# A hybrid decoder layer on one core: input projection in other passes, its norm moved behind the matmuls, the front of tile 1 and the output stages moved along the expert slots

## The reference

```python
xn = rms_norm(x, attn_norm)
proj = xn @ w_in                       # 3328 columns: q 512, k 512, v 512, p 1792
q = rope(q, pos); k = rope(k, pos)
o_da = attend(q, k, v, lam)            # differential attention, 4 heads; samples read a paged cache
o_rw, wkv, shift = rwkv_time_mix(p, shift0, wkv0, ...)   # 8 heads of 64, state carried along time
h = x + concatenate([o_da, o_rw]) @ w_out
h = h + peer_ffn(rms_norm(h, ffn_norm), peer_wq, sub_keys, peer_u, peer_v)
y = rms_norm(h, final_norm)
```

## Time and profile before

| | |
|---|---|
| median of 3 runs | 4260.41 us (4252.23 to 4271.85) |
| the profiled execution, its own time | 4256.56 us |
| its span in the profile | 4254.8 us |
| first matmul of the projection | 32.37 us |
| first expert gather (POOL) | 848.52 us |
| busy over the span | PE 68%, DVE 61%, POOL 31%, ACT 27% |
| expert gathers | 1088, 1157.7 MB of 1445.2 MB moved |
| TensorE clock granted, mean | 0.769 of full speed |

### The profile page before, as it was taken

The page is one execution under the profiler, slowest core; times in us unless marked ns, Lnnn a source line. Parts: engine busy times, 40 slices in busy tenths (PEclk is TensorE's granted clock), DMA queues, the critical chain, the costliest instruction groups (busy, mean ns, idle before and its releaser), DMA issues.

```text
span 4254.8 us, 53587 instructions
## 1 busy us (share of the span) xinstructions
...
## 2 busy tenths in 40 slices
...
DMA  7355714599999999999999999999999667999998
GB/s 259 129 174 190 264 36 167 197 401 384 418 380 408 401 412 367 413 416 379 404 413 414 378 404 406 403 379 413 403 364 387 207 233 270 355 364 419 419 410 347
DMA packets 319382, 1445.20 MB, mean 340 GB/s; under 512 B 28228, under 2 KB 64196, under 8 KB 179478
## 3 DMA queue, kind: packets, MB, share of 16 engines
...
## 4 chain that ended last, share of the span: by engine, by line
DMA 34%; PE 30%; DVE 23%; issue 5%; ACT 4%; POOL 3%; SPq 0%; DVEq 0%; ACTq 0%; POOLq 0%
DMA pe_buf<-in_experts,pe_idx 20%; DMA op_wkr<-scratch_wk_rows 10%; DVE pe_buf L2187 10%; PE ip_B L961 9%; PE pe_B L1292 4%; PE pe_psO L1342 4%; PE pe_B L1275 3%; POOL pe_buf L914 2%; PE pe_psH L1324 1%; PE pe_B L1246 1%; PE pe_B L997 1%; DMA tm_ps<-in_x 1%; ACT pe_Z L1644 1%; POOL at_vp L874 1%; DMA op_w<-in_w_out 1%
## 5 line engine op out<-in xcount | busy, mean ns | idle before, releaser
L914 POOL DMA_INDIRECT pe_buf<-in_experts,pe_idx x1088 | 1260.4, 1158 | 2750.4 <-PE pe_psO L1342 1717.0
L2187 DVE CUSTOM_DVE_ANT_0 pe_buf<-pe_buf,pe_hnR 128x1024 f32<-128x1024 f32 x1088 | 1315.1, 1223 | 886.3 <-DMA pe_buf<-in_experts,pe_idx 723.0
L1342 PE MATMUL pe_psO<-pe_buf,pe_Z 128*32 128x256 f32 x8704 | 791.6, 496 | 758.3 <-ACT pe_Z L1644 738.1
L1342 PEld LDWEIGHTS pe_psO<-pe_buf,pe_Z 128*32 128x32 f32 x8704 | 270.6, 131 | 1286.2 <-ACT pe_Z L1644 1014.6
L1636 ACT ACTIVATE pe_gelu<-pe_dot 128x2 f32<-128x2 f32 x544 | 110.2, 203 | 1678.1 <-DVE pe_dot L2187 1677.7
L961 PE MATMUL ip_B<-ip_w,ip_xT 128*128 128x512 f32 (+1 forms) x1008 | 421.7, 571 | 5.8 <-DMA ip_w<-in_w_in 4.0
L1324 PE MATMUL pe_psH<-pe_hn,pe_pick 128*128 128x512 f32 x544 | 404.0, 834 | 12.5 <-ACT pe_hnR L1606 11.0
L1292 PE MATMUL pe_B<-op_wkr,pe_mix 128*128 128x512 f32 (+1 forms) x576 | 294.9, 663 | 152.6 <-DMA op_wkr<-scratch_wk_rows 152.6
L1644 ACT ACTIVATE pe_Z<-pe_gl,pe_gelu 128x8 f32<-128x8 f32 x1088 | 267.7, 293 | 26.5 <-ACT pe_gelu L1636 1.8
L961 PEld LDWEIGHTS ip_B<-ip_w,ip_xT 128*128 128x128 f32 x1008 | 190.6, 193 | 210.8 <-issue 201.1
L1292 PEld LDWEIGHTS pe_B<-op_wkr,pe_mix 128*128 128x128 f32 (+1 forms) x576 | 115.6, 208 | 318.3 <-issue 317.8
...
## 6 DMA issues: line engine op xcount, KB each, us to landing
op_wkr<-scratch_wk_rows SPq DMA_DIRECT2D x36, 2048.0 KB, 20.8
ip_w<-in_w_in SPq DMA_DIRECT2D x24, 2048.0 KB, 8.4
op_w<-in_w_out SPq DMA_DIRECT2D x18, 2048.0 KB, 28.2
pe_buf<-in_experts,pe_idx POOLq DMA_INDIRECT x1088, 12.7
ip_w<-in_peer_wq SPq DMA_DIRECT2D x4, 2048.0 KB, 10.4
...
```

Of the source, the lines that this page charges most:

```text
L914: pool.indirect_dma_start(buf[b][:], None, T["experts"], bass.IndirectOffsetOnAxis(ap=idx[:, t % 2, h * NJ + j:h * NJ + j + 1], axis=0)).t ...
L1342: last = nc.tensor.matmul(psO[32 * x:32 * x + 32, j // 4, :], Z[:, n % NZ, 24 - 8 * turn:56 - 8 * turn], buf[n % NBUF][:, D + x * QUART:D ...
L2187: nc.vector.tensor_tensor_reduce(buf[b][:, 0:D], buf[b][:, 0:D], hnR[:, n // PH % 2, :], 1.0, 0.0, ALU.mult, ALU.add, dot[:, n % (NBUF):n ...
```

## The change

It touches the order and the projection, and computes the same.

1. `FILL` has three segments instead of four. Tile 0 is projected alone, as before; then tiles 1 and 2, the key fold and tiles 3 and 4 are one stream beside tm, at and op of tile 0; then tiles 5 to 8 beside `topk(0)`. The key fold now follows the second pass (`WK_PASS`), and the loads of keys and `peer_wq` with it.
2. tm, at and op of tile 1 move from the fill to the slots of tile 0. The list `DURING` is rotated: beside tile 0 tm, at, op of tile 1 and tm, at of tile 2; beside tiles 1 to 5 op of tile t + 1, then tm and at of t + 2; the rest (op 7, tm, at, op of tile 8) is dealt over the 128 slots of tile 6 and 76 (`LAST_OP_BY`) of tile 7, with a higher cost for the sample attention's steps.
3. `topk(t + 1)` runs in slots 42 to 122 beside tiles 1 to 6 and 80 to 122 beside tiles 0 and 7, and stands behind the front's steps in a slot.
4. The projection transposes x as loaded. The factor 1/rms goes on the rope tables (DVE, 128x128 elements) and into the scale of ACT's evictions. PE and DVE start after two constants (`first_in`); the others are waited for after tile 0's projection.
5. gelu, `Z` and `v_sum` are done for each slot alone.

```diff
 FILL = (((("ip", (0,)),),),
-        ((("wk", None), ("ip", (1, 2))), (("tm", 0), ("at", 0))),
-        ((("ip", (3, 4)),), (("op", 0),)),
-        ((("ip", (5, 6, 7, 8)),), (("tm", 1), ("at", 1), ("op", 1)), (("topk", 0),)))
-DURING = tuple((("tm", t), ("at", t), ("op", t)) for t in range(2, NT))
-COST = {"ip": 2.4, "wk": 1.8, "tm": 1.8, "at": 1.8, "op": 1.8, "topk": 1.8}
+        ((("ip", (1, 2)), ("wk", None), ("ip", (3, 4))), (("tm", 0), ("at", 0), ("op", 0))),
+        ((("ip", (5, 6, 7, 8)),), (("topk", 0),)))
+WK_PASS = 2
+DURING = ((("tm", 1), ("at", 1), ("op", 1), ("tm", 2), ("at", 2)),)
+DURING += tuple((("op", t + 1), ("tm", t + 2), ("at", t + 2)) for t in range(1, LAST - 2))
+DURING += ((("op", LAST - 1), ("tm", LAST), ("at", LAST), ("op", LAST)),)
+COST = {"ip": 3.3, "wk": 1.1, "tm": 1.9, "at": 1.3, "op": 2.2, "topk": 1.8}
+COST_LAST_AT = 3.3
+LAST_OP_BY = 76
...
-TOPK_FROM, TOPK_TO = 2, 118
+TOPK_FROM, TOPK_FROM_LAST, TOPK_TO = 42, 80, 122
...
@@ pulls
+        length = PER if t < len(DURING) - 1 else PER + LAST_OP_BY
...
@@ run
             slot(n)
             if t < LAST:
-                for _ in range(topk_pulls(k)):
-                    next(choice)
                 for _ in range(plan[n]):
                     next(front)
+                for _ in range(topk_pulls(t, k)):
+                    next(choice)
...
@@ sync, project: load of x
                     if t:
                         sp.wait_ge(ip["turned"], 2 * t)
+                        sp.wait_ge(ip["summed"], t)
+                        sp.wait_ge(ip["scaled"], t)
...
@@ tensor
-            pe.wait_ge(const_in, 16 * CONSTS_IN)
+            pe.wait_ge(first_in, 16 * FIRST_IN)
...
-                    pe.wait_ge(ip["scaled"], t + 1)
+                    pe.wait_ge(ip["x_in"], 16 * (t + 1))
...
-                if n >= 2 and n % 2 == 0:
-                    v_sum(n - 2)
+                if n:
                     v_sum(n - 1)
...
@@ scalar, project: eviction
+                            act.wait_ge(ip["scaled"], t + 1)
+                            nc.scalar.activation(ip_o[:, g_ % 2, 0, 0:cols_of(n)], ipB[:, g_ % 3, 0:cols_of(n)], ACT.Copy,
+                                                 scale=ip_r[:, 2, t:t + 1]).then_inc(ip["copied"], 1)
...
@@ scalar, slot
-                if n % 2 == 1:
-                    col = (n - 1) % (NBUF)
-                    act.wait_ge(f["dotted"], n + 1)
-                    nc.scalar.activation(gelu[:, col:col + 2], dot[:, col:col + 2], ACT.Gelu_apprx_tanh).then_inc(f["gelu_done"], 1)
+                col = n % NBUF
+                act.wait_ge(f["dotted"], n + 1)
+                nc.scalar.activation(gelu[:, col:col + 1], dot[:, col:col + 1], ACT.Gelu_apprx_tanh).then_inc(f["gelu_done"], 1)
...
@@ vector, project
-                    dve.wait_ge(ip["squared"], t + 1)
-                    chain(nc.vector.reciprocal(st[:, 2:3], st[:, 1:2]))
-                    nc.vector.tensor_scalar(ip_x[:], ip_x[:], st[:, 2:3], None, ALU.mult).then_inc(ip["scaled"], 1)
...
+                    dve.wait_ge(ip["squared"], t + 1)
+                    dve.wait_ge(ip["rope_in"], 16 * (t + 1))
+                    chain(nc.vector.reciprocal(ip_r[:, 2, t:t + 1], ip_r[:, 1, t:t + 1]))
+                    nc.vector.tensor_scalar(ip_rope[:, i].rearrange("p a d -> p (a d)"), ip_rope[:, i].rearrange("p a d -> p (a d)"),
+                                            ip_r[:, 2, t:t + 1], None, ALU.mult).then_inc(ip["scaled"], 1)
```

119 lines of the change are left out of this document (60 added, 59 removed).

## The result

The changed kernel takes 4484.51 us (median of 4 runs, 4473.94 to 4499.02) against 4261.12 us of the kernel before, measured beside it: ratio 1.0525, 95% interval 1.0486 to 1.0565. It is slower by 5.3%, where 1.0% faster was forecast. The span of the profiled execution is 4478.2 us, 223.4 more than before.

The account below looks back on a forecast made before the run. PE was taken to bound much of the fill, gathered bytes the middle tiles, with tile 6's sample attention the exception. Span 4254.8 - 113 + 48 + 0 + 25 - 1 = 4213.8, so about 4219 us measured; 8-in-10 range 4120 to 4285.

Parts of the forecast that it names:

- The fill: Stretch before the expert slots: minus 113 us in all, bounds minus 85 to minus 145.
- the start and the joints together: In the fill: earlier first matmul, minus 9 us, and less PE idle between passes, minus 10 net.
- The wait for the p rows: In the fill, DVE's 35.8 us wait for tile 0's p rows stays; nothing taken off.
- no PE joint over 25 us but the keys': Sign for the fill: PE idles over 25 us between passes only at the wait for the sub-keys.
- The rival sum by the other reading, 4185: Fill: if key-fold traffic slowed the p rows' load, its new place frees about 30 us, total 4185.
- Tiles 1 to 5, plus 0: Slots of tiles 1 to 5: same bytes, DVE's work fits under the transfers, no change; bounds minus 25, plus 75.
- DVE becomes the bound in tiles 1 to 5: Rival: chained top-k and handoffs lengthen 400 slots; at 0.35 us each plus 140, total 4360; chance 14%.
- Single gelu, costed at nothing: Slots: gelu and v sums singly free a buffer one slot earlier, which a full DMA doesn't use; no gain.
- Tile 0, plus 48: Tile 0's slots: 16 us more bytes, 32 us for DVE in slots 80 to 122; bounds plus 20, plus 80.
- Tiles 6 and 7, plus 25: Tiles 6 and 7: op of tile 7 adds 25 us, spreading the sample attention nothing; bounds minus 75, plus 80.
- the drains thin out: Rival in the sample attention: gathers cover each other, 100 us lost fall to about 20, total 4139; chance 25%.
- The third rival: No change: the fill gains less and tile 0 gives it back, total 4279; chance 13%.

Follow-up runs that it names:

- a5_front1_in_fill: The changed kernel with tile 1's front back in the fill, only tm and at of tile 2 beside tile 0; 4456.22 us, ratio 1.0479.
- a1_slots_as_before: The changed kernel with tile 1's front in the fill and the old list, costs, top-k slots and order in a slot; 4224.77 us, ratio 0.9924.
- c2_slots_before_pool_split: a1_slots_as_before with GpSimd's front steps 8 slots later and tile 0's load of 127 rows split in two; 4109.0 us, ratio 0.9678.
- b1_late_topk: The kernel before with top-k in slots 42 to 122 instead of 2 to 118; 4316.85 us, ratio 1.0134.
- a7_rotated_rest_mended: c2_slots_before_pool_split with the rotated list, its costs and its slots of top-k put back; 4247.21 us, ratio 0.9885.

## Why the prediction was wrong

**The fill: right in its sum, in part by luck.** The first gather came at 730.55 us (735 forecast). Tile 1's front was worth 101 (94 forecast, by a5_front1_in_fill against the changed kernel), the start and the joints together 8 (19 forecast, by a1_slots_as_before). The other 9 are a term that the forecast didn't have, the costs by which `merged` deals out the fill: between a1_slots_as_before and a5_front1_in_fill nothing else differs in the fill, and the first gather goes from 840.56 to 831.79 us. The first matmul came at 12.35 us instead of 23: the first weights were there sooner than I reckoned. But the next loads of weights were then the bound (9.00 us of idle at 37.14), and tile 0's projection ends about 10 us earlier, which is what the term had. The keys' wait, for which the forecast had added 21 us, shrank from 19.1 to 7.5: their load lands 4.7 us after its issue both times, but it is issued 3 us after TensorE's last matmul (at 272.13 us) and not 14 us after it (at 99.26), as before.

**The wait for the p rows: right.** It stayed, 48.1 us on VectorE in the changed kernel, as the term said; it starts 25 us earlier than before and ends 13 us earlier. TensorE idles 40.5 us by it, so the sign "no PE joint over 25 us but the keys'" didn't hold. The view of the DMA in that wait of the changed kernel, from 95 to 129 us, in 40 slices of 0.85 us (busy tenths, and rate):

```profile
DMA  0000000000000002749400000000000000000000
GB/s 25 34 25 25 25 25 25 34 25 25 25 25 25 25 25 69 269 140 348 149 19 25 25 34 25 25 25 25 25 25 25 25 34 25 25 25 25 25 25 25
```

The load of 127 rows is issued at 89.4 us and the wait for it ends at 129.6, and 25 GB/s for most of that is its 0.9 MB. The peak in the middle is q, k and v, 0.8 MB. In 112 to 128 us, where the load is alone, the window shows

```profile
112.00:128.00 16.00, 0.00 (x0) 0.00 (x0) 0.00 (x0) 0.00 (x0) 0.00 (x0) 0.50 0.06 26
```

a DMA share of 0.06, that of one engine of 16. Splitting it by rows, with the same bytes, took 28 us off the wait and 32 off the first gather. It isn't the splitting as such that helps: at 25 GB/s the part of 112 rows alone would have taken 32 us, and the wait in c2_slots_before_pool_split ends 9 us after its issue (88.4 to 97.7). So the row count is the cause. The Trainium skill, page "DMA: Bandwidth & Descriptors", section "Why a DMA increments its semaphore by 16 and not by 1", has the rule that a transfer of 127 partitions runs on one of the 16 engines; this case's trace agrees. The rival sum by the other reading, 4185, was rightly left.

**Tiles 1 to 5, plus 0: this step failed.** The prediction said: "In those 80 slots DVE has 97 + 64 + 44 = 205 us; DMA has 80 x 2.55 + 10 (w_out) = 214." The first number was good, 213.0 measured. The step from it to "nothing" was not: it set a sum of busy times against the transfers, as if VectorE could work without a pause. In tile 2 it had 30 us of waits for other engines and 7 of small gaps beside the 213, 250 in all. The two are of one queue: dots, front and top-k stand in program order, and a dot behind a waiting front step is late although its rows have landed. And the earlier trace rows, 39.2 busy of 40 us without loss, was 16 slots; that eight buffers carry such a peak is my reading, which no run isolates, but they didn't carry 80 slots. Against the 1904 us that tiles 1 to 5 take with the single gelu in the old order, the changed kernel loses 163. Shorter dots give back 119 and the order in a slot 51, together as much as the loss. The order is a clean part of it; the 119 show that VectorE's work binds, and may hold a little that the old order would have gained too. b1_late_topk shows the press alone at 49. This is the rival "DVE becomes the bound in tiles 1 to 5", which had 14%: its mechanism is the one found, the front's handoffs on top of the work. That its price of "plus 140" meets the measured +140.4 is luck: the price was 400 slots at a supposed 0.35 us, and the measured number is a loss of 163 less a gain of 23 that the forecast didn't have.

**Single gelu, costed at nothing: a gain**, of 5 to 23 us by the interval, and of 23 in tiles 1 to 5 and 12 in tile 0 by the profiled execution. It hides a part of the loss above.

**Tile 0, plus 48: mis-sized, 109.** Its slots 80 to 121 have 160.4 us of VectorE (152 forecast) in 199 (152 forecast): busy 81%, not the 95 that I had named. The same mistake again, 39 us of idle not counted. The rest is in slots 0 to 79, 282 us: two fronts, 139 steps in 73 slots. The upper bound, "plus 80", was for this, "if the front's own handoffs (139 steps in the first 73 slots, almost twice the old density) hold PE", and the measured value lies above it. The windows show one thing more. The forecast had added 16 us for the tile's 6.8 MB more of bytes, and over the whole tile these are right. But slots 0 to 79 now carry 105 MB, 15 more than before (282 us at 371 GB/s, for 226 at 398), at a DMA share of 0.95. By my estimate that is 36 of the 56 us that this part is longer, at 413 GB/s. Slots 80 to 127, where VectorE is the bound and the share is 0.71, don't give it back. Half dots and order together take only 29.5 us off this tile, so VectorE's load isn't all of its bound. In slots 0 to 79 VectorE also waits 28.5 us for ScalarE's copies of hn (L1617), 22.3 for the state of time mixing and 13.9 for one load of p rows; which of these handoffs holds the tile was not isolated and stays open.

**Tiles 6 and 7, plus 25: mis-sized, 91.** "Twelve rounds stay twelve rounds, so I take no gain and no loss from the spreading" failed. The 13 waits grew from 130.1 to 186.5 us, 14.3 a wait instead of 10.0: with 3 to 8 experts between two page gathers GpSimd is nearly always a whole set of buffers ahead, and the short rounds that were nearly free are gone. Five rounds with one or two experts took 8.4 to 12.4 us before; of the five rounds with three experts now one takes 9.3 us, the others 23.4 to 24.9. Taking the waits away gives back 128.8 us in the changed kernel and 87.7 in the old order, so 41 of the 91 are this. The other 50 is what a7_rotated_rest_mended has without those waits. The forecast had 25 of it, op of tile 7 beside tile 6. Top-k in 42 slots of tile 7, whose last 48 slots take 140 us instead of 123, is another 17; the rest was not isolated. The rival "the drains thin out" (25%) had the sign wrong: they got worse.

**The sum.** The forecast had -113 + 48 + 0 + 25 - 1 = -41. Measured on the span: -118 + 109 + 140 + 91 = +223 with the ends. The third rival, in which tile 0 gives the gain back, was true of tile 0 (it took 131 for the 101 of tile 1's front), but not of the fill, and it too had left tiles 1 to 5 at nothing.
